# First loads in column pieces and eleven zero matmuls in a two-layer decoder trunk

## What is computed

```
def rmsnorm(x, g):
    y = xf * lax.rsqrt(jnp.mean(xf * xf, axis=-1, keepdims=True) + RMS_EPS)
    return (y * g).astype(x.dtype)

for l in range(DEPTH):
    h = rmsnorm(x, mix_norm_g[l])
    z = h @ w_in[l]
    q, k, v, ch, cb, cc, ga, gc = jnp.split(z, offs, axis=-1)
    a = diff_attention(q, k, v, ...);  c = short_gated_conv(ch, cb, cc, conv_w[l])
    merged = sigmoid(ga) * (a @ w_o_attn[l]) + sigmoid(gc) * (c @ w_o_conv[l])
    x = x + merged @ w_o[l]
    h = rmsnorm(x, ffn_norm_g[l])
    x = x + (moe_swiglu(h, ...) if l % 2 else swiglu(h, ...))
return rmsnorm(x, final_norm_g)
```

## Time and profile before

| | us |
|---|---|
| median of three runs | 1665.53 |
| lowest and highest | 1664.3, 1665.89 |
| span of the profiled execution | 1661.3 |
| TensorE busy in it | 1634.2 |
| VectorE busy | 1318.2 |
| ScalarE busy | 1103.5 |

### The profile page before, as it was taken

How to read it: one execution, slowest core, us unless ns; L and a number is a source line. 1 busy time by engine, 2 the same in 40 slices (tenths; PEclk the granted TensorE clock), 3 DMA queues, 4 the chain that set the end, 5 groups by cost and what they waited for, 6 DMA issues and landing times.

```text
span 1661.3 us, 23154 instructions
## 1 busy us (share of the span) xinstructions
PE 1634.2 (98%) x8338; PEld 1371.2 (83%) x8338; DVE 1318.2 (79%) x1129; ACT 1103.5 (66%) x1081; POOL 225.4 (14%) x398
## 2 busy tenths in 40 slices
PE   9999999999999999999999999999999999999996
PEld 8988888888889888888888788887888887888875
DVE  6567656544465676469989999889999899998998
ACT  4355744434344557447768887778887688877885
POOL 0034440000000344408910000000000000000000
PEclk9999999999999999999999999999999999999999
DMA  8744554555545545537998999999999899999894
GB/s 341 267 176 152 188 180 163 205 178 200 178 178 178 178 152 181 188 139 280 414 380 336 421 421 393 413 336 398 422 404 417 347 372 422 419 403 377 349 415 206
DMA packets 71793, 488.76 MB, mean 294 GB/s; under 512 B 8651, under 2 KB 11932, under 8 KB 13212
## 3 DMA queue, kind: packets, MB, share of 16 engines
q1 hardware_dynamic: 68908, 483.37, 74.8%
q10 hardware_dynamic: 2800, 4.23, 0.7%
HBM read 484.94 MB, written 2.62 MB: 293 GB/s over the span
## 4 chain that ended last, share of the span: by engine, by line
PE 82%; DVE 10%; DMA 4%; issue 3%; ACT 1%; DVEq 0%; ACTq 0%; SPq 0%
PE bank L421 20%; PE bank L423 20%; PE bank L422 20%; DMA w_raw<-expert_slabs 4%; DVE w_lo L417 3%; PE bank L1986 3%; PE bank L1987 3%; PE bank L1756 3%; PE bank L1758 3%; PE bank L1759 3%; DVE e_uy L417 2%; DVE e_v L414 2%; PE bank L1965 2%; PE bank L2003 1%; DVE e_bias L417 1%
## 5 line engine op out<-in xcount | busy, mean ns | idle before, releaser
L417 DVE TENSOR_TENSOR w_lo<-w_raw,w_hi 128x2048 fp32r<-128x2048 f32 x288 | 654.7, 2293 | 206.7 <-ACT w_hi L408 206.2
L408 ACT ACTIVATE w_hi<-w_raw 128x2048 fp32r<-128x2048 f32 x288 | 551.3, 1918 | 392.6 <-PE bank L423 281.9
L421 PE MATMUL bank<-w_hi,hT 128*128 128x512 f32 x720 | 285.2, 396 | 1.9 <-DVE w_lo L1184 1.7
L423 PE MATMUL bank<-w_hi,hT 128*128 128x512 f32 x720 | 281.1, 390 | 0.0
L422 PE MATMUL bank<-w_lo,hT 128*128 128x512 f32 x720 | 280.7, 390 | 0.0
L421 PEld LDWEIGHTS bank<-w_hi,hT 128*128 128x128 f32 x720 | 135.4, 188 | 29.1 <-DVE hT L1173 2.5
L423 PEld LDWEIGHTS bank<-w_hi,hT 128*128 128x128 f32 x720 | 135.2, 188 | 28.6
L422 PEld LDWEIGHTS bank<-w_lo,hT 128*128 128x128 f32 x720 | 135.5, 188 | 26.5
L417 DVE TENSOR_TENSOR e_uy<-w_raw,e_k 128x2048 fp32r<-128x2048 f32 x56 | 128.3, 2290 | 16.0 <-ACT e_k L408 15.9
L414 DVE TENSOR_TENSOR e_v<-w_raw,hT 128x2048 fp32r<-128x2048 f32 x55 | 125.9, 2290 | 10.8 <-ACT hT L405 10.6
L408 ACT ACTIVATE e_k<-w_raw 128x2048 fp32r<-128x2048 f32 x56 | 107.5, 1920 | 34.5 <-PE bank L423 22.1
(11 more groups left out here) (362 smaller groups left out, 3121.8 us busy)
## 6 DMA issues: line engine op xcount, KB each, us to landing
w_raw<-expert_slabs SPq DMA_DIRECT2D x334, 1024.0 KB, 7.5
w_raw<-mix_slabs SPq DMA_DIRECT2D x88, 1024.0 KB, 4.8
w_raw<-dense_slabs SPq DMA_DIRECT2D x33, 1024.0 KB, 4.8
bias_lines<-bias ACTq DMA_DIRECT2D x1, 1536.0 KB, 8.2
X<-in_x SPq DMA_DIRECT2D x2, 512.0 KB, 5.8
bias<-bias_lines SPq DMA_DIRECT2D x1, 1024.0 KB, 6.8
yT<-in_ffn_norm_g ACTq DMA_DIRECT2D x2, 512.0 KB, 5.3
v_buf<-expert_slabs SPq DMA_DIRECT2D x1, 1024.0 KB, 4.7
```

The source lines that it names most:

```text
L408: act.activation(hi_slot(n), raw_of(n, early), ACT.Copy).then_inc(hi_ready, 1)
L417: eng.tensor_tensor(lo_slot(n), raw_of(n, early), hi_slot(n), ALU.subtract).then_inc(lo_ready, 1)
L421: pe.matmul(dst, hi, whi, start=first, stop=False, skip_group_check=True)
L423: return pe.matmul(dst, lo, whi, start=False, stop=last, skip_group_check=True)
```

## The change

The first rows of x and the norm weights are loaded in two column halves each, in the order x left, weights left, x right, weights right; each of the four transfers has its own semaphore. Half 0 is loaded in four pieces of 512 columns, each with a semaphore, and the slot's own semaphore `landed[0]` is raised by hand so that later counts hold. ScalarE's and VectorE's first operations wait for the piece that they read. The first weights no longer count in `gain_in`, so later waits on it are one load lower. Eleven zero matmuls are left of sixteen.

```
+            def first_cols(hf):
+                cols = slice(CHUNK * hf, CHUNK * (hf + 1))
+                sp.dma_start(X[:, 0, cols], x[0, 0:P, cols]).then_inc(first_x[hf], 16)
+                sp.dma_start(gain[:, cols], mix_norm_g[0, cols].partition_broadcast(P)).then_inc(first_gain[hf], 16)
+
+            def first_chunk(c):
+                cols = slice(CHUNK * c, CHUNK * (c + 1))
+                sp.dma_start(w_raw[:, 0, cols], mixer_source(0, 0)[:, cols]).then_inc(first_raw[c], 16)
+
-            sp.dma_start(X[:, 0, :], x[0, 0:P, :]).then_inc(x_in[0], 16)
-            sp.dma_start(gain, mix_norm_g[0].partition_broadcast(P)).then_inc(gain_in, 16)
-            load_half(sp, 0, mixer_source(0, 0))
+            sp.sem_inc(landed[0], 16)
+            first_cols(0)
+            first_cols(1)
+            for c in range(4):
+                first_chunk(c)
...
             def norm_sums(q, t):
-                if q == 0:
+                if q == 0 and t == 0:
+                    for hf in range(2):
+                        act.wait_ge(first_x[hf], 16)
+                elif q == 0:
                     act.wait_ge(x_in[t], 16)
...
             def first_split_hi(c):
-                act.wait_ge(landed[0], 16)
+                act.wait_ge(first_raw[c], 16)
...
             def raw_rows(q, t, hf):
+                elif t:
+                    dve.wait_ge(x_in[t], 16)
                 else:
-                    dve.wait_ge(x_in[t], 16)
-                dve.wait_ge(gain_in, 16 * (q + 1))
+                    dve.wait_ge(first_x[hf], 16)
+                if q:
+                    dve.wait_ge(gain_in, 16 * q)
+                else:
+                    dve.wait_ge(first_gain[hf], 16)
...
-            dve.wait_ge(gain_in, 16 * 5)
+            dve.wait_ge(gain_in, 16 * 4)
...
-            for _ in range(16):
+            for _ in range(11):
                 pe.matmul(bank[0][:, :], zero_r[:, 0:P], zero_r[:, :], start=True, stop=True)
```

More of the change, by code:

```diff
@@ L284, in build @@
         terms = wgtT[:, 0:2 * COLS * 2 * EXPERTS].rearrange("p (r c e) -> p r c e", r=2, c=COLS)
-        x_in = [sem(f"x_in{t}") for t in range(TT)]
+        x_in = {1: sem("x_in1")}
+        first_x, first_gain = ([sem(f"{n}{hf}") for hf in range(2)] for n in ("first_x", "first_gain"))
+        first_raw = [sem(f"first_raw{c}") for c in range(4)]
         relb_in, bucket_in, lam_in, sub_in, conv_in, rtr_in, gain_in = (
```

## The result

| | before | changed |
|---|---|---|
| median of 13 runs each, us | 1665.25 | 1667.64 |
| lowest and highest | 1663.99, 1666.82 | 1665.64, 1671.0 |
| ratio, 95% interval | | 1.0016 [1.0009, 1.0024] |
| profiled execution: span | 1661.3 | 1667.5 |
| TensorE begins half 1 | 17.61 | 19.82 |

The profiled execution of the changed kernel took 1669.24 us, 1.7 above its span. If as much lies around the span of before, that execution took about 1663.0, a quick one among its runs. So 6.2 us between the spans overstate the change; 2.4 us between the medians is the figure. It also means that the 3.0 to 4.6 us above the span, read earlier as what lies around the first and last instruction, were for the most part the difference between one quick execution and three others: 1.7 to 1.8 us lie around the span in every execution that has both figures.

The account below looks back on a forecast made before the run. TensorE, busy 1634.2 of 1661.3 us, was taken as the bound. Its first matmul's 1.7 us gain shrinks through two landing waits to 0.2 at half 1 (17.61 to 17.42), giving 1665.3 us, range 1662.8 to 1667.3.

Parts of the forecast that it names:

- the landing of half 1: First loads: half 1 lands at 12.94 us as before; finer transfers shift it between -0.8 and +0.6, taken as zero.
- x and the weights in column halves: First loads: first halves land by about 4.5 to 5 us, second halves at 6.5 as before, or everything behind 0.8 sooner.
- The term for the pieces of half 0: Half 0's load: chunks land near 7.15, 7.8, 8.4 and 9.0 us; a slower rate makes it up to 0.4 late.
- the prediction's own sign: Forecast is wrong if half 1's split starts far from 13.0, later matmuls are 0.43 apart, or the shift is lost later.
- if halves moved like lam_qk: Norm weights at the start: at the 362 GB/s of lam_qk they take 1.45 us, everything behind lands near 0.8 sooner.
- the fixed price per transfer: Load queue: 0.12 us each, bounded by three small transfers behind half 1; 0.6 for five added ones.
- The place where it is decided: Everything is decided before 17.6 us, where TensorE starts half 1; a shift there is carried to the end.
- A low clock before 14 mostly costs nothing, as TensorE waits there anyway: TensorE before 14 us: running at 1.2 GHz there was expected to cost mostly nothing.
- alone this is worth nothing: Five fewer zeros at TensorE's start, ending at 6.55 instead of 8.10 us: no gain alone, since other waits cover it.
- rival C: TensorE's clock stays at 1.2 GHz after eleven zeros: short stretch 1.5 us slower (0.08), long up to 7.4 (0.05).
- I expect full clock from about 7 to 8: TensorE's start: with eleven zeros, 2.4 GHz was expected from about 7 to 8 us, judged from a stretch at the router.
- B: Rival: small pieces cost, half 1 lands up to 0.6 us late, kernel 0.4 slower, 1665.9; chance 0.16.

Follow-up runs that it names:

- e12: Kernel before with half 1, not half 0, loaded in four pieces of 512 columns; half 1 landed at 13.05 us, against 12.97 before.
- e3: Kernel before with only half 0 loaded in four pieces of 512 columns; half 1 landed at 13.96 us, TensorE began it at 18.37.
- e3b: Second profile of the kernel before with only half 0 in four pieces; half 1 landed at 13.76 us, TensorE began it at 18.16.
- e4: Kernel before with eleven zero matmuls, not sixteen, as only edit; TensorE began half 1 at 18.93 us, not 17.61.
- e9b: Kernel before with eleven zeros ahead of the first transposes and five behind; TensorE began half 1 at 17.38 us; ratio 1.0000 [0.9991, 1.0009].
- b1: Kernel before with norm weights loaded as one row and spread by TensorE matmuls, zeros rearranged; half 1 begun at 19.91 us; ratio 1.0012 [1.0003, 1.0021].
- e11: Kernel before with only the first rows of x in two column halves; half 1 landed at 15.88 us, TensorE began it at 21.55.
- e1: Changed kernel with the norm weights whole again; half 1 landed at 14.61 us; ratio to before 1.0008 [0.9999, 1.0017], median 1666.49.
- e2: Kernel before with only the norm weights in two column halves; half 1 landed at 13.98 us; ratio 1.0008 [0.9999, 1.0017], median 1667.39.
- e8: Kernel before with the first norm-weight load replaced by 128 rows of x; these landed at 5.85 us, half 1 at 12.44; whole run 1788.58.
- e6: Kernel before with half 0 in four transfers of 32 partitions each, whole 8 KB rows; half 1 landed at 15.51 us.

## Why the prediction was wrong

The range ended at 1667.3 and the median is 1667.64. The direction was wrong too: 0.2 us faster was forecast, 2.4 slower came.

*The step that failed* is the landing of half 1: "they nearly cancel (faster weights, slower chunks), and I take zero", between ends of -0.8 and +0.6. It was +2.44, and +2.21 at TensorE's start on half 1 is the whole of the loss in the medians within their spread. Within it, the term that failed is the one of x and the weights in column halves: "the second half lands when everything did, 6.5", or up to 0.8 sooner. It landed at 8.43, 1.93 later. The term for the pieces of half 0 held, with 0.17 where 0.4 was allowed; that half 1 itself took 0.35 longer stood in no term. By the prediction's own sign, a start of half 1's split far from 13.0, the forecast is wrong: ScalarE's copy of it started at 15.44. Three things were wrong in the pricing. The slow weights were priced by bytes ("if halves moved like lam_qk"), when each half took about as long as the whole had. The nearest row was taken from 15 us, in a queue that ran steadily, though the trace showed that the same kind of transfer at 4 us ran at 293 GB/s and not 362. And the fixed price per transfer, 0.12, came from that steady stretch as well; e12 shows at most 0.2 for three more there, and e3 and e3b show that three more in the first microseconds cost 0.7 to 1.0.

*What held.* The place where it is decided held: half 1's landing, copy, split and start, all with the durations of the earlier trace rows (1.91, 2.29), and the shift at 17.6 was found at 740. Zeros ended at 6.26, transposes came in two groups, VectorE's first product was sooner, at 5.58. VectorE waited for the second rows as foreseen, 1.28 us and not 0.9, two microseconds later. The first real matmul did not move (10.60 against 10.64): the right weights at 8.43 stood before it.

*The clock.* "A low clock before 14 mostly costs nothing, as TensorE waits there anyway" was wrong, and so was "alone this is worth nothing" for the five zeros, although neither decided this result. e4 shows 1.3 us by a path through three queues that the working of rival C did not have; C had priced a stretch of low clock at 1.5 (its own sum, 0.2 + 6 x 0.2, gives 1.4). And the zeros were not "nearly half" of TensorE's 11.37 us before 14.76 but more: they ran from 1.49 to 8.10, 6.6 us. "I expect full clock from about 7 to 8" missed what counts: it rose sooner, at 5.8, and fell again at 9.2 in the gap, which the working had not looked at. By the Trainium skill (TensorE: Matmul & The Clock Gate, What's actually happening) activity releases the throttle. The profiles agree in part: in e4 the level fell at 10.19, after TensorE had worked 1.17 us since 6.8, and in e9b, with five zeros more in that gap, it stayed; but in b1 TensorE was busy from 1.49 on and the level rose only at 13.18.

*The rivals.* B had the direction, finer transfers that cost, with a quarter of the size, and it looked for the cost in the pieces of half 0 and in their number. In the change most of it lies ahead of them. The Trainium skill (DMA: Bandwidth & Descriptors, Bandwidth) advises large batches; for the start of this kernel that pointed the right way. Paid in series, the 2.0 us for each transfer of the Trainium skill (same page, Anatomy of one DMA) would have given 10 us by the prediction's estimate, and the profiles show 2.44 for the five together, and 0.8 to 2.9 for single parts.

*Open.* Why a row broadcast at the start disturbs what surrounds it, so that splitting x alone cost 2.9 us in its one profile, was not found. The profiles show only that packets take longer there: 122 ns and not 84 in the change, up to 1.6 us in e11. e11 was profiled once, and e1 and e2 too. Nor was it tried whether the order matters, x left, x right and then the weights, or the weights further back in the queue.

## What to carry to other kernels

In this kernel a transfer cut in pieces was nearly free only where the queue ran steadily; at a start, price each piece by a row of that same place, and a broadcast by the time it took, not by its bytes. Before a gap filler is taken away, look through every queue for what stands behind the first work after the gap. And when loads are bound by the queue, an earlier first piece buys nothing if the last one comes later.

## What the runs showed that was not expected

- One row of 4 KB sent to 128 partitions took 1.6 to 2.4 us at the start, 128 different rows 1.27 (e8). In halves with x between them it took 2.0 and 2.3, in adjacent halves 2.3 and 0.7 (e2).
- 32 partitions in 8 KB rows moved at 214 GB/s (e6), 128 partitions at about 419: packets took about 600 and 309 ns.
- Float32 products with a single row of data, zeros and transposes, in all 9 us without a break, left the clock at 1.2 GHz until 13.2 (b1). With zeros alone it had risen between 4.7 and 7.5 in the profiles with sixteen ahead of the transposes.
- Between the two profiles of the kernel before, the start of the same VectorE instructions in the experts' stage wanders by 3.8 us.
